# Second layer's scores in three products of the rounded format, of queries and keys split in high and low parts

## The reference

```
proj = rmsnorm(x) @ w_in;  q, k, v, gate = split(proj, 4)
for each block of 128 queries (qpos), all keys (key_pos):
    mask = key_pos < qpos
    z = einsum('qd,sd->qs', q_blk, k) * D ** -0.5
    log_1m = where(mask, log_sigmoid(-z), 0)
    tail = cumsum(log_1m, reverse=True) - log_1m
    A = where(mask, exp(log_sigmoid(z) + tail), 0)
    o = A @ v
x = x + (o * silu(gate)) @ w_out;  out = rmsnorm(x)
```

## Time and profile before

| | us |
|---|---|
| median of 3 runs | 1374.46 |
| lowest and highest | 1374.28, 1375.1 |
| span of the profiled execution | 1372.5 |

### The profile page before, as it was taken

How to read it: one execution, slowest core, us unless ns; L and a number is a source line. 1 busy time by engine, 2 the same in 40 slices (tenths; PEclk the granted TensorE clock), 3 DMA queues, 4 the chain that set the end, 5 groups by cost and what they waited for, 6 DMA issues and landing times.

```text
span 1372.5 us, 18983 instructions
## 1 busy us (share of the span) xinstructions
PE 1327.3 (97%) x7213; PEld 1076.1 (78%) x7213; DVE 972.7 (71%) x1687; ACT 675.3 (49%) x1018; POOL 554.9 (40%) x372
## 2 busy tenths in 40 slices
PE   7998999999999999999998999999999999998997
PEld 5786888888888888887886678777777878776786
DVE  5587788879787979876337856777767677777413
ACT  6354436363635445364226555556555655655203
POOL 6432334333334333332224785636365563622300
PEclk9999999999999999999999999999999999999999
DMA  7210110111102120206213211112221111119403
GB/s 195 79 36 16 31 47 16 47 47 47 47 17 62 31 62 20 61 22 223 81 43 127 89 31 31 47 47 65 66 55 47 46 47 47 46 46 306 170 1 123
DMA packets 106859, 91.46 MB, mean 67 GB/s; under 512 B 3105, under 2 KB 92306, under 8 KB 106770
## 3 DMA queue, kind: packets, MB, share of 16 engines
q1 hardware_dynamic: 106770, 90.25, 21.7%
HBM read 66.65 MB, written 23.59 MB: 66 GB/s over the span
## 4 chain that ended last, share of the span: by engine, by line
PE 80%; DVE 12%; ACT 4%; issue 3%; DMA 0%; POOL 0%; DVEq 0%; SPq 0%; ACTq 0%
PE psum L518 25%; PE psum L673 17%; PE psum L687 5%; PE psum L2462 4%; PE psum L2436 4%; PE psum L2381 2%; PE psum L2449 2%; DVE terms L1871 2%; PE psum L2369 2%; PE psum L535 2%; PE psum L2347 2%; DVE stick L2019 2%; PE psum L646 2%; PE psum L2322 1%; DVE small_L L1856 1%
## 5 line engine op out<-in xcount | busy, mean ns | idle before, releaser
L518 PE MATMUL psum<-u_hi,w_hi 128*128 128x512 f32 x640 | 260.6, 407 | 3.9 <-DVE u_lo L1583 1.7
L518 PE MATMUL psum<-u_hi,w_lo 128*128 128x512 f32 x640 | 259.0, 405 | 0.0
L518 PE MATMUL psum<-u_lo,w_hi 128*128 128x512 f32 x640 | 258.3, 404 | 0.0
L485 POOL TENSOR_TENSOR w_lo<-w_raw,w_hi 128x1024 fp32r<-128x1024 f32 (+1 forms) x45 | 107.7, 2394 | 251.5 <-ACT w_hi L480 239.2
L518 PEld LDWEIGHTS psum<-u_hi,w_hi 128*128 128x128 f32 x640 | 120.8, 189 | 31.3 <-issue 4.3
L518 PEld LDWEIGHTS psum<-u_hi,w_lo 128*128 128x128 f32 x640 | 120.8, 189 | 25.8 <-issue 1.9
L518 PEld LDWEIGHTS psum<-u_lo,w_hi 128*128 128x128 f32 x640 | 121.1, 189 | 22.1 <-issue 0.5
L1726 DVE SCALAR_TENSOR_TENSOR late<-raw,cols,late 128x1024 f32<-128x1024 f32 x72 | 129.1, 1793 | 1.8
L615 POOL TENSOR_TENSOR w_lo<-w_raw_b,w_hi 128x512 fp32r<-128x512 f32 x40 | 52.7, 1319 | 136.2 <-ACT w_hi L599 136.2
L2019 DVE TENSOR_TENSOR_SCAN stick<-soft 128x1024 f32<-128x1024 f32 (+3 forms) x64 | 103.6, 1618 | 0.2
L480 ACT ACTIVATE w_hi<-w_raw 128x1024 fp32r<-128x1024 f32 (+1 forms) x45 | 45.8, 1019 | 110.1 <-PE psum L518 109.9
(11 more groups left out here) (302 smaller groups left out, 3224.8 us busy)
## 6 DMA issues: line engine op xcount, KB each, us to landing
w_raw<-in_a_w_in SPq DMA_DIRECT2D x33, 512.0 KB, 4.1
w_raw<-in_b_w_in SPq DMA_DIRECT2D x16, 512.0 KB, 5.5
w_raw_b<-in_b_w_in SPq DMA_DIRECT2D x16, 512.0 KB, 5.6
b_rows<-o_part SPq DMA_DIRECT2D x14, 512.0 KB, 3.8
o_rows<-o_part_a SPq DMA_DIRECT2D x12, 512.0 KB, 3.6
x_stage<-in_x SPq DMA_DIRECT2D x8, 512.0 KB, 7.3
out<-fin_o SPq DMA_DIRECT2D x8, 512.0 KB, 2.6
u_lo<-b_rows SPq DMA_DIRECT2D x7, 512.0 KB, 8.2
```

Source lines behind the costliest of these rows:

```text
L485: G.tensor_tensor(lo_tiles(key), raw_tiles(key), hi_tiles(key).bitcast(F32), ALU.subtract).then_inc(lo_done, 1)
L518: mm = PE.matmul(psum[:, half], (w_hi, w_hi, w_lo)[part][:, buffer(key), k], (u_hi, u_lo, u_hi)[part][:, k, half * HALF:(half + 1) * HALF] ...
```

## The change

`scale_qk` now multiplies in place in `b_raw`, in one piece of 1024 columns for the keys and one for the queries, in step 4. Two functions are new. `qk_upper` on ACT copies keys and queries with rounding into `k_hi` and `q_hi`, tokens 128 to 1023 after `softplus` of step 4's turn and tokens 0 to 127 after that of step 5's. `qk_lower` on DVE subtracts these to give `k_lo` and `q_lo`, the large part before `mask` of step 5's turn and the small part behind `scan`. `scores` takes three products for each stretch of keys in place of one plain float32 matmul: 288 products in place of 96 matmuls. For block 4 the keys are cut in 384 and 256 in place of 512 and 128, by starting 128 columns into the PSUM slot. In the first head's preparation one group of 12 products now stands ahead of the scores. The buffer `o_part` (and the use of `o_row`) is half as long, so that both halves of the outputs pass through the same place: `gate_out` waits for the store of the half before. `b_g` moves to another place in memory.

```diff
--- before.py
+++ after.py
...
@@ -721,6 +728,14 @@
 
         FIN_BEHIND = {TAIL[9 + n]: n for n in range(4)}
 
+
+        def scored(s):
+
+            qb = Q_BLOCKS[s]
+            start = P if qb == 4 else 0
+            return banks(2 + 2 * (s % 2))[:, start:start + (qb + 1) * P]
+
+        QK_PARTS = (slice(P, T), slice(0, P))
 
         def in_all(fill):
             return [sum(fill[:s + 1]) for s in range(len(fill))]
@@ -920,7 +935,7 @@
             def store_b(h, part_no):
                 half = 1 - part_no
                 sp.wait_ge(bo_lo, 2 * h + part_no + 1)
-                sp.dma_start(b_rows[h][:, :, half_range(half)], o_part[:, :, half_range(half)].bitcast(F32)).then_inc(b_out[half], 16)
+                sp.dma_start(b_rows[h][:, :, half_range(half)], o_part[:, :, :].bitcast(F32)).then_inc(b_out[half], 16)
 
             def load_b(k):
                 for half in range(2):
@@ -1216,9 +1231,8 @@
 
             def output_upper(h, part_no):
 
-                t = half_range(1 - part_no)
                 bo_done.wait(act, h, part_no + 1)
-                A.activation(o_part[:, 1, t], o_row[:, 0, t], ACT.Copy).then_inc(bo_hi, 1)
+                A.activation(o_part[:, 1], o_row[:, 0, 0:HALF], ACT.Copy).then_inc(bo_hi, 1)
 
             def take(key, half, dst):
                 act.wait_ge(proj_ready, FIRST[key] + half + 1)
@@ -1489,15 +1503,26 @@
             for f in range(4, 6):
                 ended_pair(f)
 
+            def qk_upper(h, i):
+
+                part = QK_PARTS[i]
+                qk_scaled.wait(act, h, 2)
+                if h == 0:
+                    act.wait_ge(res_out, 16 * (KB - HOME + KB))
+                else:
+                    sc_ready.wait(act, h - 1, NC - 1 + i)
+                A.activation(k_hi[:, part], b_raw[:, 1, part], ACT.Copy).then_inc(qk_hi.handle, 1)
+                A.activation(q_hi[:, part], b_raw[:, 0, part], ACT.Copy).then_inc(qk_hi.handle, 1)
+
             def weights(h, s):
                 w, slot = (Q_BLOCKS[s] + 1) * P, s % 2
                 arg_done.wait(act, h, s + 1)
                 A.activation(stick[:, slot, 0:w], stick[:, slot, 0:w], ACT.Exp).then_inc(a_done.handle, 1)
 
             def softplus(h, s, last_weights=False):
-                w, slot, bk = (Q_BLOCKS[s] + 1) * P, s % 2, 2 + 2 * (s % 2)
+                w, slot = (Q_BLOCKS[s] + 1) * P, s % 2
                 mask_done.wait(act, h, s + 1)
-                A.activation(soft[:, slot, 0:w], banks(bk)[:, 0:w], ACT.Abs).then_inc(soft_a.handle, 1)
+                A.activation(soft[:, slot, 0:w], scored(s), ACT.Abs).then_inc(soft_a.handle, 1)
                 if last_weights:
                     weights(h - 1, NC - 1)
                 soft_a.wait(act, h, s + 1)
@@ -1528,13 +1553,15 @@
                         softplus(h, s + 2)
                     elif follow:
                         softplus(h + 1, s + 2 - NC, s == NC - 2)
+                    if s in (4, 5) and follow:
+                        qk_upper(h + 1, s - 4)
                     if not follow and s == 0:
                         split_hi(("out", 1))
                     fill.to(STEP_AT[2 * s + 1])
                     if s == 1:
                         gn_done.wait(act, h, 1)
                         bo_done.wait(act, h - 1, 2)
-                        A.activation(b_g[:, :], b_raw[:, 2], ACT.Silu).then_inc(bg_done.handle, 1)
+                        A.activation(b_g, b_raw[:, 2], ACT.Silu).then_inc(bg_done.handle, 1)
                         A.preload_act_table_set(LN_EXP)
                     if s == 0 and follow and h > 0:
                         output_upper(h - 1, 1)
@@ -1547,6 +1574,8 @@
                         split_hi(("out", 3))
                 fill.to(2 * PAIR - GROUP)
 
+            for i in range(2):
+                qk_upper(0, i)
             softplus(0, 0)
             for f in range(6, 10):
                 ended_pair(f)
@@ -1650,9 +1679,8 @@
 
             def output_lower(h, part_no):
 
-                t = half_range(1 - part_no)
                 dve.wait_ge(bo_hi, 2 * h + part_no + 1)
-                V.tensor_tensor(o_part[:, 0, t], o_row[:, 0, t], o_part[:, 1, t].bitcast(F32), ALU.subtract
+                V.tensor_tensor(o_part[:, 0], o_row[:, 0, 0:HALF], o_part[:, 1].bitcast(F32), ALU.subtract
                                 ).then_inc(bo_lo, 1)
 
             def rms_by_tokens(rnd):
@@ -1986,13 +2014,21 @@
                     input_lo("p6", j - 1)
             input_lo("p6", HALF_KB - 1)
 
-            def scale_qk(h, part):
+            def scale_qk(h):
                 dve.wait_ge(pair_act, 4 * h + 4)
                 if h > 0:
                     dve.wait_ge(pair_dve, 10 * h)
-                V.scalar_tensor_tensor(out=b_q[:, part], in0=b_raw[:, 0, part], scalar=float(P) ** -0.5,
-                                       in1=rsb[:, part], op0=ALU.mult, op1=ALU.mult).then_inc(bqk_done.handle, 1)
-                V.tensor_tensor(b_k[:, part], b_raw[:, 1, part], rsb[:, part], ALU.mult).then_inc(bqk_done.handle, 1)
+                V.tensor_tensor(b_raw[:, 1], b_raw[:, 1], rsb[:, :], ALU.mult).then_inc(qk_scaled.handle, 1)
+                V.scalar_tensor_tensor(out=b_raw[:, 0], in0=b_raw[:, 0], scalar=float(P) ** -0.5,
+                                       in1=rsb[:, :], op0=ALU.mult, op1=ALU.mult).then_inc(qk_scaled.handle, 1)
+
+            def qk_lower(h, i):
+
+                part = QK_PARTS[i]
+                for n, (lo, hi) in enumerate(((k_lo, k_hi), (q_lo, q_hi))):
+                    qk_hi.wait(dve, h, 2 * i + n + 1)
+                    V.tensor_tensor(lo[:, part], b_raw[:, 1 - n, part], hi[:, part].bitcast(F32), ALU.subtract
+                                    ).then_inc(bqk_done.handle, 1)
 
             def scale_v(h, half):
                 vt_ready.wait(dve, h, half + 1)
@@ -2002,14 +2038,14 @@
 
             def mask(h, s):
                 qb = Q_BLOCKS[s]
-                diag = banks(2 + 2 * (s % 2))[:, qb * P:(qb + 1) * P]
+                diag = scored(s)[:, qb * P:(qb + 1) * P]
                 sc_ready.wait(dve, h, s + 1)
                 V.tensor_tensor(diag, diag, causal[:, :], ALU.min).then_inc(mask_done.handle, 1)
 
             def softplus_sum(h, s):
-                w, slot, bk = (Q_BLOCKS[s] + 1) * P, s % 2, 2 + 2 * (s % 2)
+                w, slot = (Q_BLOCKS[s] + 1) * P, s % 2
                 soft_c.wait(dve, h, s + 1)
-                V.scalar_tensor_tensor(out=soft[:, slot, 0:w], in0=banks(bk)[:, 0:w], scalar=0.0,
+                V.scalar_tensor_tensor(out=soft[:, slot, 0:w], in0=scored(s), scalar=0.0,
                                        in1=soft[:, slot, 0:w], op0=ALU.max, op1=ALU.add
                                        ).then_inc(sp_done.handle, 1)
 
...
@@ -2036,9 +2072,9 @@
             def gate_out(h, part_no):
                 half = 1 - part_no
                 t = slice(half * HALF, (half + 1) * HALF)
-                dst = o_row[:, 0, t] if h < H - 1 else o_raw[:, h, t]
-                if 1 <= h < H - 1:
-                    dve.wait_ge(b_out[half], 16 * h)
+                dst = o_row[:, 0, 0:HALF] if h < H - 1 else o_raw[:, h, t]
+                if h < H - 1 and (h, part_no) != (0, 0):
+                    dve.wait_ge(b_out[1 - half], 16 * (h + part_no))
                 av_ready.wait(dve, h, (4, 8)[part_no])
                 bg_done.wait(dve, h, 1)
                 V.tensor_tensor(dst, psum[:, 7], b_g[:, t], ALU.mult).then_inc(bo_done.handle, 1)
@@ -2086,17 +2122,19 @@
                     fill.to(STEP_AT[2 * s])
                     softplus_sum(*ahead)
                     if s == 5:
-                        scale_qk(h + 1, slice(P, T))
+                        qk_lower(h + 1, 0)
                     if s + 2 < NC:
                         mask(h, s + 2)
-                        if s == 5:
-                            scale_qk(h + 1, slice(0, P))
+                        if s == 4:
+                            scale_qk(h + 1)
                     else:
                         mask(h + 1, s + 2 - NC)
                     if s == NC - 1:
                         fill.to(STEP_AT[2 * s + 1] - GROUP)
                         copy_aT(h, s, 0)
                     scan(*ahead)
+                    if s == 5:
+                        qk_lower(h + 1, 1)
                     if s == 0:
                         scale_v(h, 0)
                     if s < NC - 1:
@@ -2117,11 +2155,11 @@
 
             dve.sem_inc(bo_done.handle, 2)
 
-            dve.wait_ge(res_out, 16 * (KB - HOME + KB))
             dve.wait_ge(nrs_done, 2)
-            for part in (slice(0, 2 * P), slice(2 * P, T)):
-                scale_qk(0, part)
+            scale_qk(0)
             ended_pair(5)
+            for i in range(2):
+                qk_lower(0, i)
             dve.wait_ge(consts, CONSTS_A + 2)
             mask(0, 0)
             ended_pair(7)
@@ -2430,11 +2468,14 @@
                         pair_products(2 * h + p, lo, hi)
 
             def scores(h, s):
```

(16 more changed lines are left out.)

20 lines of the change are left out of this document (13 added, 7 removed).

## The result

| | before | after |
|---|---|---|
| median, us | 1374.37 | 1399.76 |
| lowest and highest | 1374.17, 1375.1 | 1399.1, 1400.8 |
| span of the profiled execution | 1372.5 | 1398.0 |

The ratio is 1.0187, with an interval of 1.0175 to 1.0200: 25.4 us more, where 17.3 were forecast. The mean granted clock of the profiled execution is 0.986.

A forecast was written before the change was run, and what follows sets the result against it. PE's own work sets the pace, with no DVE slack in steps 5 and 6. Heads 11.3, first head 4.7, clock 1.5 and last head -0.3 sum to 17.2, from 1372.5 to 1389.7, median 1391.7 us; range 1380 to 1402.

The forecast's parts named there:

- first rival: The clock falls at the heads' stalls too, 1.5 us each, 10.5 more over seven heads: 1402; 13%.
- PE's part: Scores on PE: 128 columns priced at 0.23, block 0 at 0.69 us; a head saves 0.97 (1.31 with the floor).
- The chain of steps 4 and 5: DVE from block 1's mask to its `exponent`: 12.1 us from 9.2; next head's first scores 2.77 later.
- the replay: DVE's changed steps 4 and 5 worked through on one head's times, added operations waiting for POOL: 1.6 us a head.
- What a head gives back: Net head period: 2.35 late less 0.73 from blocks 5 to 2, so 1.6 us longer; +11.3 over seven heads.
- The 0.42 from the mask nearer to the scores: DVE's chain behind a head's first scores starts 0.42 us closer to them, 1.37 in place of 1.79.
- The clock: Lower clock level after the first head's stall, 1.5 us once; nothing added at the heads' stalls of 2.2.
- The first head: DVE's four subtractions each meet POOL and end at 804.9; PE stands for 5.3 us; net +4.7.
- The rest: Last head -0.3 us for shorter scores; halved `o_part` costs nothing; ACT's copies hidden except where told.
- Products no cheaper: Rival: three products no cheaper than the plain one, or the wait eats the gain exactly: 1374.5; 5%.
- PE never waits: Rival: DVE's added operations fit in the idle 2.24 us, a head saves 0.97: 1368, faster; 8%.
- POOL slips past: Rival: POOL's operations slip past DVE's; net 0.4 us a head, 1.0 at the start, no clock fall: 1378; 12%.

The follow-up runs named there:

- x_best: Changed kernel, plain first scores in head 0, earlier scaling, small subtractions behind step 5's `exponent`, step 7's take earlier, pair products reshared: 1366.12 us, ratio 0.9946.
- x_no_low: Changed kernel without DVE's four subtractions; all three products read high parts: 1367.15 us, ratio 0.9953.
- x_plain: Changed kernel with plain float32 matmuls of the high parts for the scores, all else kept: 1407.63 us, ratio 1.0244.
- x_start: Changed kernel, head 0's first scores one plain float32 product at the place of before, their mask ahead of the subtractions: 1393.96 us, ratio 1.0152.
- x_fill: Changed kernel with pair products reshared: three more in step 5, two more in step 6, five fewer in step 7: 1397.39 us, ratio 1.0170.
- x_scale_early: Changed kernel with the scaling ahead of step 4's mask in place of behind it: 1383.67 us, ratio 1.0071.
- x_pool_short: Changed kernel with POOL's subtractions for the weights' low parts cut to 4 of 128 columns from the 12th factor on: 1395.35 us, ratio 1.0151.
- x_half: Kernel before with only `o_part` halved and the waits that go with it: 1374.21 us, ratio 1.0002.
- x_before_fill: Kernel before with pair products reshared (three more in step 5, two more in step 6, five fewer in step 7): 1374.00 us, ratio 0.9996.

## Why the prediction was right, and where it was small

The sign, the place and the mechanism held, and 1399.76 lies in the range of 1380 to 1402, near its end. It is nearer to the first rival's 1402 than to the 1391.7 forecast, since the errors of the four parts point the same way. By its steps:

- **PE's part.** The price of 128 columns was taken from the wrong end: 992.25 to 992.36 is 0.11, the floor, and block 0 costs 0.35 or a little less (in x_best 0.28 from its first product at 974.05 to the transposes at 974.33), not 0.69. The four passes that the prediction inferred from two products of 64 columns don't show. A head saves 1.3 to 1.4, not 0.97. The 0.34 more did no good in the changed kernel, since PE waits behind block 0: the stall was 2.40 for 2.2. Only in x_best, where PE is the bound, it counts; the 1.52 won there is up to 0.2 more than the products explain.
- **The chain of steps 4 and 5** was 12.17, replayed as 12.1, and from the scores of block 1 (986.41) to the next head's first (999.28) it is 12.87 us where it was 9.96: 2.91 more, replayed as 2.77. The 0.14 are twice 0.07: the earlier trace rows have a DVE operation of 896 columns end 0.95 behind POOL's end, and the replay took 0.88 for it (measured 0.95), and 1.01 for 1024 columns (1.08). This is the step on which the forecast rested. Both meetings with POOL came where the replay put them (1.81 and 1.93). The Trainium skill, "SBUF — State Buffer", "SBUF: two separate sides", says that whichever of the two starts first has the ports for the whole instruction. The page names, for DVE, operations with two inputs in SBUF; here the scans have two as well (the buffer `soft` twice). The trace agrees, in both directions, and for scans too: 3.38 for 2.09 on DVE, 4.12 for 2.39 on POOL.
- **What a head gives back** is where the size went wrong: 1.6 forecast, 2.3 measured, 0.14 of the difference from the chain. The 0.42 from the mask nearer to the scores was won and lost at once, in the scan of block 0. The replay had no POOL operation there, but there was one before the change already:

```profile
986.60 0.74 DVE L2019 TENSOR_TENSOR_SCAN stick<-soft 128x128 f32<-128x128 f32 x1
```

```profile
985.78 1.28 POOL L615 TENSOR_TENSOR w_lo<-w_raw_b,w_hi 128x512 fp32r<-128x512 f32 x1 [5.46 <-ACT w_hi L599]
```

It ends 2.66 behind the first scores at 984.40, as L622 does with the change (1001.94 behind 999.28), and the scan ends 2.94 behind them in both. An earlier mask only makes the scan stand longer, 1.06 for 0.74. So block 6's scores came 3.51 behind block 7's, as before, instead of 3.08; in x_no_low, where the scan stood free (0.41), it is 2.79. With the change the scan met POOL in six heads of seven (0.56 to 1.53). And block 5's 0.25 was lost since the interval to block 4's scores was 11.24, as before (11.25): there DVE sets the pace. The blocks 4 to 2 gave 0.22, 0.29 and 0.11. Over six periods this is 4.2 of the 8.3 us missing.
- **The clock** was said not to fall at the heads (the rival, with 13%, said it would, at 1.5 each). It fell in five of seven, and cost 1.24 twice: 2.5 us. The rival had the fall right and its price by luck: it reckoned products at half speed, and the 1.24 is a meeting of DVE and POOL. With the chain longer than either had it, the result lies between the two. The Trainium skill, "TensorE: Matmul & The Clock Gate", "Why this matters for your kernels", warns of longer idle gaps between bursts. The trace agrees for the 5.20 us; the gaps of 2.40 are shorter than those that the page warns of, and there the measurement decides. By the runs, gaps of 2.39 to 2.42 were enough in five heads of seven in the changed kernel, in x_plain and in x_start alike, 15 of 21, and gaps of 1.10 to 1.72 in none of the 21 heads of x_fill, x_scale_early and x_pool_short. Why six were spared stays open.
- **The first head.** The chain ended at 804.35 (forecast 804.9), PE stood for 5.20 (5.3), and the four subtractions each met POOL:

```profile
798.06 1.69 DVE L2030 TENSOR_TENSOR k_lo<-b_raw,k_hi 128x896 fp32r<-128x896 f32 x1 [0.81 <-ACT k_hi L1514]
799.68 2.15 DVE L2030 TENSOR_TENSOR q_lo<-b_raw,q_hi 128x896 fp32r<-128x896 f32 x1
801.75 1.34 DVE L2030 TENSOR_TENSOR k_lo<-b_raw,k_hi 128x128 fp32r<-128x128 f32 x1
803.01 1.34 DVE L2030 TENSOR_TENSOR q_lo<-b_raw,q_hi 128x128 fp32r<-128x128 f32 x1
```

The 128 columns that take 0.29 alone took 1.34 twice. Up to the second head's first scores 7.8 were forecast and 8.97 measured; the forecast had 3 us at the lower clock after the earlier trace rows, and it was 5.8, up to 810.2:

```profile
810.12 0.60 PE L680 MATMUL psum<-t_lo,w_hi 128*128 128x512 f32 x1
810.55 0.41 PE L680 MATMUL psum<-t_hi,w_lo 128*128 128x512 f32 x1
```

Products are 0.43 apart up to there, and 0.23 with the full clock.

- **The rest.** The halved buffer is free (x_half). The last head was +0.1 for -0.3. "Products no cheaper" and "PE never waits" are both refuted by x_no_low and the waits; "POOL slips past" by the 1.81 and 1.93.

Together: 17.2 and 4.2 (heads), 2.5 (clock at heads), 1.2 (start) and 0.4 (end) make 25.5. The start's part is the least certain: before's first scores came at 796.85 in this execution and at 794.83 in that of x_before_fill, whose code is the same up to there.

## What to carry to other kernels

Work that is cheaper on the engine that sets the pace is only a gain if the preparation that it needs on another engine has room before the point where the first one waits: look for that engine's idle time in front of that point, and put what waits for nothing there and what waits for a third engine behind it. With nearly the same instructions in another order (the first head's first scores alone went back to plain float32) the change went from 1.9% slower to 0.5 to 0.7% faster. Where two engines meet on shared memory, look for the next meeting before you shorten or move one of the two: in x_pool_short, x_scale_early and x_start the meeting came back at another operation. And a stall that is filled on one engine came back at its next wait (x_fill), since the other engine's chain was the bound.

## What the runs showed of the chip

- A rounded product of 128 columns starts 0.11 us after the one before it, nearly as one of 256 (0.12); two of 64 columns, by the 0.39 that they last together, are 0.11 apart as well. Below 256 columns the width saves next to nothing.
- A scan with its inputs in SBUF stands beside POOL as a subtraction does: 128 columns 0.41 alone, 0.56 to 1.53 with POOL, 384 columns 0.94 and 1.82, 896 columns 2.09 and 3.38.
- Behind a stall of 2.4 us the granted clock can fall, and this cost 1.24 us where DVE's scan of block 0 then came behind the start of POOL's next operation, and nothing where it came 0.3 us earlier (x_start shows the same). In x_plain, where the plain products are the longer part, it cost 1.2 to 1.5 though the scans lasted only 0.41 to 0.57.
- The first head's scores of identical code started at 794.83 and at 796.85 in two profiled executions: a difference of 2 us ahead of them is not a result.
